# A two-layer fp32 transformer: gate and up products by Strassen's scheme, down products in parts of four row tiles

## The reference, cut to what matters

```python
def swiglu(h, w_gate, w_up, w_down):          # 1024 -> 2816 -> 1024
    return (jax.nn.silu(h @ w_gate) * (h @ w_up)) @ w_down

for l in range(DEPTH):
    mx = (jax.nn.silu(c) @ w_mod[l] + b_mod[l]).reshape(B, N_MOD, 1, D)
    x = x + 0.5 * mx[:, 2] * swiglu(modulate(rms_norm(x), mx[:, 0], mx[:, 1]), ...)
    ...token mixing of latent and context tokens, residual gated by mx[:, 5]...
    x = x + 0.5 * mx[:, 8] * swiglu(modulate(rms_norm(x), mx[:, 6], mx[:, 7]), ...)
```

## Time and profile before

| | us |
|---|---|
| median of 3 runs | 2996.32 |
| lowest, highest | 2994.11, 2999.31 |
| the profiled execution's own time | 2992.3 |
| its span | 2990.3 |
| PE busy in the span | 2887.6 (97%) |
| VectorE busy | 1597.5 (53%) |
| ScalarE busy | 947.2 (32%) |
| GpSimd busy | 267.5 (9%) |
| granted PE clock, mean | 0.992 of 2.4 GHz |

### The profile page before, as it was taken

How to read it: one execution, slowest core, us unless ns; L and a number is a source line. 1 busy time by engine, 2 the same in 40 slices (tenths; PEclk the granted TensorE clock), 3 DMA queues, 4 the chain that set the end, 5 groups by cost and what they waited for, 6 DMA issues and landing times. The chain is left out here.

```text
span 2990.3 us, 44352 instructions
## 1 busy us (share of the span) xinstructions
PE 2887.6 (97%) x16733; PEld 2701.8 (90%) x16733; DVE 1597.5 (53%) x2877; ACT 947.2 (32%) x1521; POOL 267.5 (9%) x272
## 2 busy tenths in 40 slices
PE   7999999999989899999999999999998989999999
PEld 3999999978978789999999899999997978888887
DVE  5665366453467746643664566346235577633332
ACT  3221122132368732211122321112223368532222
POOL 1000000022213300000000100000003124100000
PEclk9999999999999999999999999999999999999999
DMA  5343234222100223332432244233213201223333
GB/s 202 120 122 107 87 112 138 80 61 58 48 13 4 70 71 115 118 103 69 130 115 87 74 125 136 60 96 117 77 53 87 62 13 32 84 84 107 88 96 95
DMA packets 413317, 263.01 MB, mean 88 GB/s; under 512 B 11086, under 2 KB 404724, under 8 KB 413200
## 3 DMA queue, kind: packets, MB, share of 16 engines
q1 hardware_dynamic: 410128, 256.86, 28.9%
q10 hardware_dynamic: 2432, 4.46, 0.4%
q0 software_dynamic: 640, 0.09, 0.0%
HBM read 255.08 MB, written 2.10 MB: 86 GB/s over the span
## 5 line engine op out<-in xcount | busy, mean ns | idle before, releaser
L422 PE MATMUL pair<-h_hi,w_hi 128*128 128x384 f32 (+1 forms) x2656 | 919.1, 346 | 11.8 <-DVE w_lo L396 11.8
L423 PE MATMUL pair<-h_lo,w_hi 128*128 128x384 f32 (+1 forms) x2656 | 908.7, 344 | 0.0
L426 PE MATMUL pair<-h_hi,w_lo 128*128 128x384 f32 (+1 forms) x2656 | 733.0, 344 | 0.0
L422 PEld LDWEIGHTS pair<-h_hi,w_hi 128*128 128x128 f32 x2656 | 499.9, 188 | 39.5 <-issue 7.3
L423 PEld LDWEIGHTS pair<-h_lo,w_hi 128*128 128x128 f32 x2656 | 500.3, 188 | 21.2
L396 DVE TENSOR_TENSOR w_lo<-w_raw,w_hi 128x1024 fp32r<-128x1024 f32 (+1 forms) x266 | 350.5, 1318 | 286.3 <-ACT w_hi L389 282.9
L426 PEld LDWEIGHTS pair<-h_hi,w_lo 128*128 128x128 f32 x2656 | 477.8, 188 | 16.2
L389 ACT ACTIVATE w_hi<-w_raw 128x1024 fp32r<-128x1024 f32 (+1 forms) x271 | 302.2, 1117 | 541.0 <-PE pair L426 513.3
L422 PE MATMUL pair<-s_hi,w_hi 128*128 128x384 f32 (+1 forms) x1100 | 378.4, 344 | 0.0
L423 PE MATMUL pair<-s_lo,w_hi 128*128 128x384 f32 (+1 forms) x1100 | 377.7, 343 | 0.0
L865 DVE SCALAR_TENSOR_TENSOR mod_acc<-mod_raw,cs,mod_acc 128x256 f32<-128x256 f32 x896 | 366.3, 481 | 0.0
(11 more groups left out here) (256 smaller groups left out, 3804.9 us busy)
## 6 DMA issues: line engine op xcount, KB each, us to landing
mod_raw<-in_w_mod SPq DMA_DIRECT2D x64, 1024.0 KB, 5.0
w_raw<-in_w_ffn_gate SPq DMA_DIRECT2D x88, 512.0 KB, 3.8
w_raw<-in_w_ffn_up SPq DMA_DIRECT2D x88, 512.0 KB, 3.8
w_raw<-in_w_ffn_down SPq DMA_DIRECT2D x64, 704.0 KB, 4.6
w_raw<-in_w_in SPq DMA_DIRECT2D x32, 512.0 KB, 3.9
w_raw<-in_w_out SPq DMA_DIRECT2D x12, 512.0 KB, 3.8
w_raw<-in_w_q_up SPq DMA_DIRECT2D x8, 576.0 KB, 4.5
mod_first<-in_w_mod ACTq DMA_DIRECT2D x4, 1024.0 KB, 14.4
```

Source lines behind the costliest of these rows:

```text
L422: eng.matmul(dst, wh, rh, start=first, stop=False)
L423: eng.matmul(dst, wh, rl, start=False, stop=False)
L426: last = eng.matmul(dst, wl, rh, start=False, stop=end)
```

## The change

**Gate and up products.** A matrix of 1,024 x 256 weights (two hidden tiles of gate, or of up; called a unit) is cut into four blocks of 512 x 128, and the normed tokens into four blocks of 512 features x 384 tokens (256 in the last FFN block). Seven products of such blocks give the unit's four result blocks, by the Winograd form of Strassen's scheme. The products are named p1 to p7. p1 and p2 take weight blocks and token blocks as they are; the others take weight differences (`T_NAMES`: t1 to t4, GpSimd, `ff_t`, L1123), token sums and differences (`s1` to `s4`, once per FFN block, `form_s1` to `form_s4`), or both. Their results are combined out of PSUM: p6, p7 and p4 accumulate in one bank that VectorE reads between them (`ff_event`, L1638), and ScalarE keeps a copy of p1 (`snapshot`). An operand that is a sum is split into high and low part after it is formed. Here `OPS` is the order of products, `u` the unit, `ff_lo` (L1154) the low part of an operand, on VectorE or GpSimd by `lo_on_pool`.

**Down products.** The 22 hidden tiles are taken in parts of 4, 4, 4, 2, 4, 4 (`FF_PARTS`, in units of two), in place of two halves of 11. After each part eight output tiles run over its chunks and are added to `xT`, so each output tile is added six times in place of two.

**Around it.** Modulation goes two instructions per product and four per output tile of a part (`mod_room`), in place of 16 per tile of hidden features. Weights are loaded in slabs of 1,024 x 256 (1 MB) into two slots; high and low parts go through a ring of six. All loops are written out. The seam between FFN blocks now takes six output tiles in token halves, and the second half of the tokens is normed while the first products run (`ff_open_dve`, L1671, and its counterparts).

```diff
+FF_PARTS = (2, 2, 2, 1, 2, 2)
+PRODUCTS = ("p1", "p6", "p2", "p7", "p5", "p4", "p3")
+OPENING = [(0, "p1"), (1, "p1"), (0, "p2"), (1, "p2")] + [(u, x) for u in range(2) for x in ("p6", "p7", "p5", "p4", "p3")]
+SLOTS = 6
+HI_LEAD, LO_LEAD, T_LEAD = 5, 4, 8
+def lo_on_pool(inst, i):
+    if not is_unit(OPS[i]) or OPS[i] in ((0, "p5"), (0, "p3")):
+        return False
+    return OPS[i][1] in (("p2", "p5") if inst == N_FF - 1 else ("p2", "p5", "p3"))
...
+def mod_room(i):
+    if not is_unit(OPS[i]):
+        return 2 if FF_PARTS[OPS[i][1]] == 2 else 0
+    return 0 if OPS[i - 1][1] == "p3" and OPS[i - 1][0] % 2 and i > 40 else 1
...
+        def ff_t(eng, inst, u, name):
...
+            a, b = {"t3": (raw_block(u, 1, 1), raw_block(u, 0, 1)), "t1": (raw_block(u, 0, 1), raw_block(u, 0, 0)),
+                    "t2": (raw_block(u, 1, 1), raw_block(u, 0, 1)), "t4": (raw_block(u, 1, 0), t_view(u, "t2"))}[name]
+            eng.tensor_tensor(t_view(u, name), a, b, ALU.subtract).then_inc(f_t, 1)
...
+        MOVING = {"p3": "s4", "p4": "a22", "p5": "s1", "p6": "s2", "p7": "s3"}
...
+        def unit_op(eng, inst, i):
+            u, x = OPS[i]
+            wait_lo_of(eng, inst, i)
+            if x in ("p1", "p6", "p5"):
+                wait_bank(eng, inst, u, x)
+            elif x == "p2":
+                eng.wait_ge(f_snap, inst * 2 * FF_PAIRS + u + 1)
+            else:
+                eng.wait_ge(f_event, event_count(inst, u, {"p7": "u2", "p4": "a", "p3": "c22"}[x]))
+            dst = chain(inst, u, CHAIN_OF[x])
+            for k in range(KH):
...
+                last = part_product(eng, k, stationary(inst, i), moving(inst, x, k), dst, k == 0 and x in ("p1", "p6", "p5"),
...
-                        eng.tensor_tensor(into, up, gate, ALU.mult).then_inc(acc_free[(o + 1).odd], 1)
-                        eng.wait_ge(s_hi_done, s.n(1))
-                        eng.tensor_tensor(s_lo[:, bass.ds(i, 1), 0:w].rearrange("p a t -> p (a t)"), sf[:, 0:w],
...
+            for i in range(8, N_OPS + 1 if last else END + 1):
+                op = OPS[i - 1]
+                mod_dve(eng, inst, i) if i < N_OPS and not is_unit(op) else None
+                if not is_unit(op):
+                    down_residual(eng, inst, i - 1)
+                elif event_of(op):
+                    ff_event(eng, inst, op[0], event_of(op))
+                while lo <= min(i + LO_LEAD, N_OPS - 1):
+                    ff_lo_dve(eng, inst, lo)
+                    lo += 1
+                if op[1] == "p3" and op[0] % 2:
+                    mult_last(eng, inst, op[0] // 2)
+                mod_dve(eng, inst, i) if i < N_OPS and is_unit(op) else None
```

More of the change, by code:

```diff
@@ L123 @@
 for _l in range(DEPTH):
[L124 to L134, removed]
@@ L617, in part_products @@
-        def part_products(eng, o, chunks, lhs, rhs, a, b, before=None, done=None):
-            for k in range(chunks):
-                if before:
-                    before(k)
-                part_product(eng, o, k, lhs, rhs, a, b, k == 0, k == chunks - 1, done)
-        def part_product(eng, o, k, lhs, rhs, a, b, first, end, done):
-            (wh, wl), (rh, rl), dst = lhs(k), rhs(k, a, b), pair[o.odd][:, a:b]
-            eng.matmul(dst, wh, rh, start=first, stop=False)
-            eng.matmul(dst, wh, rl, start=False, stop=False)
-            last = eng.matmul(dst, wl, rh, start=False, stop=end)
-            if end and done is not None:
-                last.then_inc(done, 1)
@@ L667, in open_pe, with cross_pool, mix_open_pe @@
+        def cross_pool(eng, q):
+            n = len(tail_tiles(q))
+            for e in range(n):
+                if e < n - 1:
+                    tail_add(eng, q, 1, e)
+                for k in chunks_by(q, e):
+                    norm_lo_pool(eng, q, 0, k)
+        def mix_open_pe(eng, q, tiles, cols):
+            at, inst, parts = chunks_at(q), norms[q]["after"], norm_parts(q)
             for k in range(KD + LAG):
@@ L687, in open_pe @@
[L687 to L689 removed]
+                eng.wait_ge(f_res, residual_count(q, 1, 5))
+                for k in range(KD):
+                    wait_low(eng, at + KD + k + 1)
+                    a, b = parts[1]
+                    last = part_product(eng, k, first_tile(j), h_moving(k, a, b), pair[o.odd][:, a:b], k == 0, k == KD - 1)
+                last.then_inc(acc_done, 1)
@@ new lines, in ff_sp @@
+            for h in range(2 if pairs else 0):
+                mod_load(eng, pairs[0], h)
+            n = 2
+            for i in range(N_OPS):
+                while n < len(RAWS) and RAW_LAST[n - 2] - LO_LEAD <= i:
+                    ff_load(eng, inst, n)
+                    n += 1
+                for v, k in MOD_STEPS[inst].get(i, ()):
+                    if k % KH == KH - 1 and v + 1 in pairs:
+                        mod_load(eng, v + 1, k // KH)
+            first_loads(eng, following)
@@ L1274, in mix_pe @@
             for i0, i1 in ((0, 1), (1, KD // 2 - 1)):
-                for i in steps(eng, i0, i1):
+                for i in range(i0, i1):
                     for j in range(2):
@@ L1359, in mix_sp @@
             eng.wait_ge(a_out, (ATT_C0[l] + 6 * nb) // 2)
-            for i in steps(eng, 1, KD // 2):
+            for i in range(1, KD // 2):
                 for j in range(2):
@@ L2189, in _ @@
             mod_turn(pe)
+            for p in range(2):
+                norm_spread(pe, X_NORM[0, 0], p)
             for b in blocks:
```

1411 lines of the change are left out of this document (958 added, 453 removed), and 4 rows, old and new, of the table FF_SEGS.

## The result

| | before | changed |
|---|---|---|
| median of the runs, us | 2995.93 (4 runs) | 3142.19 (4 runs) |
| lowest, highest | 2994.11, 2999.31 | 3138.52, 3144.12 |
| profiled span | 2990.3 | 3136.6 |
| granted PE clock, mean | 0.992 | 0.96 |

The ratio is 1.0485, 95% interval 1.0467 to 1.0504: 4.9% slower. The forecast was 3140 us.

A forecast was written before the change was run, and what follows sets the result against it. TensorE, busy 97%, bounds the kernel before; after the change VectorE, blocked by GpSimd, paces modulation. Terms 119 - 24 + 8 + 5 + 24 + 12 = +144 take 2992.3 to 3136, plus 4 gives 3140 us; eight-in-ten range 2888 to 3235.

The forecast's parts named there:

- modulation pairs: First three FFN blocks, 23.6 pairs (14 gate and up products each) with modulation: 38.0 us against 32.97 before, +119 us.
- openings: Starts of FFN blocks: idle TensorE 14 us against some 4, less 4.1 saved; three at +6, last about +6: +24.
- pairs without: First three FFN blocks, 6.4 pairs of gate and up products without modulation: 29.2 us each, -24 us in all.
- last block's pairs: Gate and up products of the last FFN block: 22.5 us a pair against 21.7 before, 10 x 0.8 = +8 us.
- down tiles: Down products with modulation: eight output tiles take 33.5 us against 33.0, 10.8 such groups, +5 us.
- single-pair part: Part with one pair: no first chunks cover the chain combination, product, rounding, low part; 3 us x 4 = +12.
- Products saved: Seven gate and up products for eight: -136.0 us in the first three blocks, -18.8 in the last; alone 2837.5 us.
- The exclusion: VectorE's instructions with two SBUF tensors and GpSimd's exclude each other while streaming; modulation pair between 30.9 and 42.8 us.
- 17 x 0.82 = 13.9 us: VectorE's delay per modulation pair: 17 GpSimd instructions, each holding 1.10 us with 0.28 covered, on top of 24.1 us.
- Idle 14: Opening, before the first unit's p3: VectorE needs 31 us, TensorE's eight products last 16.5, so 14 us idle.
- The floor rival: GpSimd runs where VectorE reads PSUM: modulation pairs at 31 to 35 us, whole 2974 to 3069 us; chance 0.18.
- The rival by which TensorE stays the bound: Exclusion narrower than read, VectorE's 24.1 and GpSimd's 21.1 us fit under TensorE's 28.85 a pair: 2891 us; chance 0.25.

The follow-up runs named there:

- e2: Changed kernel with GpSimd's FFN differences, low parts and products cut to 8 columns after each block's first two units (computes something else): 2952.1 us.
- e5: Kernel before the change, with GpSimd work that nothing reads added in the second and third FFN blocks: 3013.7 us.
- e6: Changed kernel with each GpSimd weight difference and low part cut into two instructions of 256 elements, same result: 3080.9 us.
- e1: Changed kernel with 14 of a tile pair's 16 modulation instructions per half cut to 8 columns in the FFN blocks (computes something else): 3075.5 us.
- e3: Changed kernel with the cuts of e1 and e2 together (computes something else): 2945.0 us.
- e7: Changed kernel with the third block's modulation moved: none in the opening pair, then at two of three products, same result: 3132.4 us.
- e4: Changed kernel with all low parts of weight operands on VectorE, none on GpSimd in the FFN, same result: 3125.5 us.
- e9: Changed kernel with GpSimd's weight differences and low parts of the first three blocks cut into four instructions of 128 elements, same result: 3078.2 us.

## Why the prediction came out right

By its own steps; "measured" is from the rows above and the like parts of the other blocks. That the total matches to 2 us is luck: the modulation pairs came 62 us under the forecast, the openings 46 over, and 21 us stand in no term.

| term | forecast | measured |
|---|---|---|
| modulation pairs, 23.6 | +119 (38.0 us each) | +57 (35.4) |
| pairs without, 6.4 | -24 (29.2) | -22 (29.3 to 29.9) |
| last block's pairs | +8 (22.5) | +11 (22.2, one part 25.0) |
| down tiles, per eight | +5 (33.5) | +5 (34.2 less 0.7 of transposes) |
| single-pair part | +12 | +4 |
| openings | +24 | +70 |
| left over | 0 | about +21 |

- **Products saved.** Right. The part without modulation takes 58.6 us for 57.7 of bare starts (336 x 0.1717).
- **The exclusion.** Right in kind, shown by e2, e5 and e6; with GpSimd's work gone the modulation parts lose their stall entirely. The size was off in "17 x 0.82 = 13.9 us": the plan's 17 GpSimd instructions a pair include 3 that fall beside the down products, which I charged there again, and a meeting costs 0.73. 14 x 0.73 = 10.3. VectorE's own share was 23.2 (half of e2's 46.45), forecast 24.1; with 2.2 us of idle VectorE the pair takes 35.7, and 35.4 without the transposes. The choice of 38.0 also rested on a slip: the middle of 30.9 and 42.8 is 36.9, which would have given +93.
- **Why 0.73 and not 0.82.** Not settled by a run. That the wait does not depend on the size of the VectorE instruction (e1) and shrinks with GpSimd's (0.91, 0.51 and 0.23 us for 512, 256 and 128 elements) fits waiting out the one in progress.
- **Openings.** The step that failed is where the sum for them ends, at the first unit's last product (p3). Up to there it was good: "Idle 14" is three gaps of 5.2, 3.2 and 7.8 us, 16.1, and most of them stay in e2 and e3. Behind it three more follow, 1.1, 2.8 and 9.6, which the sum has at nothing. Left out were (1) modulation steps inside the opening, two per product from 1192.69 us on, which e7 prices at 9.4 us; (2) the transposes that wait for them in TensorE's queue, 9.2 us there, so the same load once more; (3) the clock: with the gaps of 5.2, 3.2 and 7.8 us, and again with that of 9.6, the granted clock falls to 0.50 (1.2 GHz), and 38 matmuls start 0.33 us apart in place of 0.172, 6.1 us in this opening (7.6 in the third block's). The opening took 90.4 us against 70.8 for the same tiles before, so +19.6, of which 2.4 belong to its second pair: 17.2 x 3, and 18 in the last block. (e3's "bare 57.7" counts 336 matmuls; 24 of them run ahead of the stretch, so it holds 312, 53.6 us.)
- **Seams.** The seam of 51.4 us between the second and third block has TensorE busy 43.9 at clock 0.91, 7.5 us idle against 3.4 in the earlier trace rows. With 18 matmuls at half clock (2.8 us) that is 7 us more than before in this seam, and TensorE's idle time ahead of the second block's opening is 7.3 us against 3.4. The 21 us left over are a remainder, not taken apart further; these are among them.
- **Single pair, down products, transfers.** The part of 33.9 us is cheaper than half a double one (36); the following down products pay 3.5 us for it. Down products matched. No wait of TensorE in the FFN is put down to a transfer: those of the weights cost nothing, as said.
- **What was to be seen.** In the third row's stretch PE under 85%: missed, 88%. VectorE over 90%: 94%. Steps at about 0.9 us: 0.85. Low parts at about 1.1: missed, 0.83. GpSimd above 1.29: 1.46 for its low parts. TensorE at 95% without modulation: 100%.

The floor rival (pairs at 31 to 35 us) was missed by 0.4 us: by pairs alone it was nearly the better case, and with openings as forecast and nothing left over the kernel would have come out near its upper end of 3069. The rival by which TensorE stays the bound fell with the result; e2 and e4 show why. There the Trainium skill's rule (Perfetto Trace Analysis, Identifying the Most-Contended Engine) to read occupancy as distance from the limit fails for these two engines, since a blocked instruction shows as busy: in a modulation part VectorE is busy 67.0 of 71.4 us, and for the same instructions 46.5 in e2.

A version that wins was not found. By rows, an estimate: with all of GpSimd's FFN work free (e2) the gain over before is 42 us; its openings of 76 to 78 us, for matmuls worth 53.6, take back over 20 us each in the second and third block. A first pair by eight plain products, with the sums formed beside it, would aim at that. It was not tried.

## What to carry to other kernels

Before moving work to GpSimd, count VectorE's instructions with SBUF inputs beside it and, where VectorE is as full of them as here, charge each GpSimd instruction some 0.7 us of VectorE time at 512 elements; if it must go there, try pieces of 256, with an eye on GpSimd's own busy time (e6's last block and e9). Price the start of each block apart from its steady state, with every wait that stands in TensorE's own queue and the slower clock after it. And a sum that comes out right proves none of its terms: check them by stretches.

## What the hardware showed that I had not expected

- The one-input step `TENSOR_SCALAR` (L1020) is blocked too: 0.342 us where no GpSimd instruction runs (93 times), 1.10 on average where one does (35 times), up to 1.41. I had read "two SBUF tensors" as the condition. The Trainium skill (SBUF — State Buffer, Who interferes with whom) lists it among the operations that can take the shared pair, and describes the pair as an exclusive lock held for an instruction; the trace agrees with both (the 27 of these that are held up end 0.15 us after the end of a GpSimd instruction).
- An instruction of 8 columns waits as long as one of 256 (e1).
- Splitting GpSimd's instructions raises its busy time and lowers the kernel's (e6: +9 us of GpSimd, -6 us, in one part).
- Idle TensorE costs twice: the gaps of an opening, and 6.1 us lost to matmuls at 1.2 GHz after them.
